# Residual spill behind two more loads, and the first pair of block products made ready inside the opening, in a two-block transformer kernel on Trainium2

## The reference, cut to what matters

```python
def rms_norm(x, g):
    y = x * lax.rsqrt(jnp.mean(x * x, axis=-1, keepdims=True) + RMS_EPS)
    return y * g
...
x = x + rms_norm(mixed @ w_out[l], norm_mix_post[l])
h = rms_norm(x, norm_ffn_pre[l])
f = (jax.nn.silu(h @ w_ffn_gate[l]) * (h @ w_ffn_up[l])) @ w_ffn_down[l]
x = x + rms_norm(f, norm_ffn_post[l])
```

## Time and profile before

| | |
|---|---|
| median of 3 runs | 1445.99 us (1445.91 to 1446.22) |
| the profiled execution's own time | 1444.36 us |
| its span | 1442.6 us |
| TensorE busy | 1414.1 us, 98% |
| VectorE, ScalarE, GpSimd busy | 812.2, 716.8 and 793.2 us |
| DMA | 143.03 MB, 99 GB/s over the span |
| granted TensorE clock, mean | 0.995 |

### The profile page before, as it was taken

How to read it: one execution, slowest core, us unless ns; L and a number is a source line. 1 busy time by engine, 2 the same in 40 slices (tenths; PEclk the granted TensorE clock), 3 DMA queues, 4 the chain that set the end, 5 groups by cost and what they waited for, 6 DMA issues and landing times.

```text
span 1442.6 us, 22205 instructions
## 1 busy us (share of the span) xinstructions
PE 1414.1 (98%) x8248; PEld 1207.4 (84%) x8248; DVE 812.2 (56%) x1426; ACT 716.8 (50%) x1254; POOL 793.2 (55%) x462
## 2 busy tenths in 40 slices
PE   9999999999999988899999999999999999999999
PEld 7888888888788767799998887877677899999887
DVE  6425656776525266676763345888765667764000
ACT  5143435665644235566652225665666566664221
POOL 4434323762344426877764456766237877775443
PEclk9999999999999999999999999999999999999999
DMA  6423312122133322332324333422124423233433
GB/s 204 137 87 88 88 59 59 45 60 59 52 97 100 97 108 78 113 117 89 118 86 148 105 110 126 127 74 59 45 73 146 124 96 118 91 115 117 126 108 117
DMA packets 40050, 143.03 MB, mean 99 GB/s; under 512 B 4656, under 2 KB 4912, under 8 KB 39696
## 3 DMA queue, kind: packets, MB, share of 16 engines
q1 hardware_dynamic: 38688, 139.08, 31.0%
q10 hardware_dynamic: 1264, 2.62, 0.6%
HBM read 135.40 MB, written 6.29 MB: 98 GB/s over the span
## 4 chain that ended last, share of the span: by engine, by line
PE 87%; DVE 5%; POOL 3%; ACT 2%; issue 2%; DMA 1%; SPq 0%; DVEq 0%; ACTq 0%; POOLq 0%
PE bank L1596 10%; PE bank L1598 10%; PE bank L1597 10%; PE bank L1949 8%; PE bank L1951 8%; PE bank L1950 8%; PE bank L1625 3%; PE bank L1627 3%; PE bank L1626 3%; PE bank L2053 3%; PE bank L2055 2%; PE bank L2054 2%; PE bank L1843 1%; PE bank L1878 1%; PE bank L1863 1%
## 5 line engine op out<-in xcount | busy, mean ns | idle before, releaser
L671 POOL TENSOR_TENSOR wL<-raw,wH 128x1024 fp32r<-128x1024 f32 x165 | 404.8, 2453 | 518.9 <-ACT wH L848 387.4
L848 ACT ACTIVATE wH<-raw 128x1024 fp32r<-128x1024 f32 x136 | 143.7, 1057 | 322.3 <-PE bank L1598 251.2
L1596 PE MATMUL bank<-aH,wH 128*128 128x512 f32 x376 | 150.1, 399 | 14.3 <-POOL wL L671 14.3
L1597 PE MATMUL bank<-aL,wH 128*128 128x512 f32 x376 | 147.7, 393 | 0.0
L1598 PE MATMUL bank<-aH,wL 128*128 128x512 f32 x376 | 147.6, 393 | 0.0
L1596 PE MATMUL bank<-fH,wH 128*128 128x512 f32 x352 | 137.1, 389 | 0.0
L1598 PE MATMUL bank<-fH,wL 128*128 128x512 f32 x352 | 137.1, 389 | 0.0
L1597 PE MATMUL bank<-fL,wH 128*128 128x512 f32 x352 | 137.0, 389 | 0.0
L1949 PE MATMUL bank<-aH,wH 128*128 128x256 f32 x408 | 115.3, 283 | 0.0
L1951 PE MATMUL bank<-aH,wL 128*128 128x256 f32 x408 | 115.3, 283 | 0.0
L1950 PE MATMUL bank<-aL,wH 128*128 128x256 f32 x408 | 115.2, 282 | 0.0
(11 more groups left out here) (456 smaller groups left out, 3844.8 us busy)
## 6 DMA issues: line engine op xcount, KB each, us to landing
raw<-in_w SPq DMA_DIRECT2D x200, 512.0 KB, 3.6
raw_too<-in_w SPq DMA_DIRECT2D x34, 512.0 KB, 3.8
kept_x<-xT SPq DMA_DIRECT2D x2, 2048.0 KB, 9.2
xT<-kept_x SPq DMA_DIRECT2D x8, 512.0 KB, 4.9
bmk<-in_bias SPq DMA_DIRECT2D x6, 512.0 KB, 4.7
out_x<-xT SPq DMA_DIRECT2D x8, 256.0 KB, 4.6
xT<-in_x SPq DMA_DIRECT2D x3, 512.0 KB, 7.0
ct<-in_ct ACTq DMA_DIRECT2D x3, 384.0 KB, 3.7
```

The costliest lines, as they stand in the source:

```text
L671: pool.tensor_tensor(wL[:, c_slot, :], raw[:, c_slot, :], wH[:, c_slot, :].bitcast(F32), ALU.subtract).then_inc(sem("w_lo"), 1)
L848: act.activation(wH[:, s, :], raw[:, s, :], ACT.Copy).then_inc(sem("w_hi"), 1)
L1596: pe.matmul(bank[:], hi, H[:, ka, :], start=(k == 0), stop=False)
L1597: pe.matmul(bank[:], hi, L[:, ka, :], start=False, stop=False)
```

## The change

Both gu stages are changed in the same way, as far as the first has it differently from the second.

1. **Spill.** The store of the residual is cut into two halves of 1 MB. In gu1 they stand behind loads 5 and 6 of the phase, in gu2 behind loads 3 and 4; before, one store of 2 MB stood behind load 3.
2. **y_work.** The tile is moved in memory (fH is placed first), and in gu1 the eight `y_made` copies are issued one by one behind the copies that make aH, before the squares; before, they stood in two groups of four behind the first and the second feature. gu2 had them early already.
3. **POOL in gu1.** The four `t_sum` and three `t_low` are put one by one between the lows of chunks 3 to 10; before, they came from chunk 7 on, some in twos. In gu2 the `t_low`s move one chunk back. The `t_high`s on ACT follow.
4. **First pair.** It lands in raw_too instead of raw (all pairs change slots), and its loads wait for the spill and for the users of xT instead of for the lows of the last two opening chunks. Its x11 is split before the last chunk's copy, its x21 copied, s1 and s3 split before x12, and p5(0) is computed between p1(0) and p2(0) instead of between p1(1) and p4(0). ACT's `keep_u2(0)` stands ahead of the copy of pair 1's x21.
5. **Down phase.** Since the last pair now lies in raw, the first two chunks of dn wait for its s4 and its x22 instead of for those of the pair before it.

Core of the diff (orders of waits in `pair_orders` follow the code and are left out, as is the matching reorder in DVE's `swiglu`, which takes s1's low and s4 of pair 0 ahead of the loop):

```diff
@@ two_blocks_kernel @@
+            fH = sb("fH", [P, KF, S], F32R, ffn)
             with ExitStack() as over:
-                sb("under_y", [P, KF - KD, S], F32, over)
+                sb("under_y", [P, KF - 2 * KD, S], F32, over)
                 y_work = sb("y_work", [P, KD, S], F32, over)
-            fH = sb("fH", [P, KF, S], F32R, ffn)
...
-            return raw_too[:, tile, :] if j % 2 else raw[:, (early + tile) % 2, :]
+            return raw[:, (early + tile) % 2, :] if j % 2 else raw_too[:, tile, :]
@@ SP, pair_loads @@
-                for tile in range(2):
-                    sp.wait_ge(sem("w_lo"), p.c0 + p.nt - 1 + tile)
-                    pair_load(p, 0, tile)
-                sp.wait_ge(sem("stored"), 16 * (stage_of(p) + 1))
+                sp.wait_ge(sem("stored"), 32 * (stage_of(p) + 1))
                 sp.wait_ge(sem("pair_act"), after("y_made", KD * (stage_of(p) + 1)))
...
@@ SP, down_loads @@
+                    if c == 0:
+                        sp.wait_ge(sem("pair_dve"), after("s4", done))
+                    if c == 1:
+                        sp.wait_ge(sem("pair_pool"), after("lo_x22", done))
@@ SP, openings @@
-                        if t == 3:
+                        if t in ((5, 6) if p.name == "gu1" else (3, 4)):
...
-                            sp.dma_start(kept, xT[:].rearrange("p a s -> p (a s)")).then_inc(sem("stored"), 16)
+                            kt = 0 if t in (3, 5) else KD // 2
+                            sp.dma_start(kept[:, kt * S:(kt + KD // 2) * S], xT[:, kt:kt + KD // 2, :].rearrange("p a s -> p (a s)"))\
+                                .then_inc(sem("stored"), 16)
@@ ACT, before gu1 @@
-            high_of_x("h2", "g_ffn_pre", "res1", None, kts=range(0, 4))
-            ahead(PH["gu1"], 0)
-            high_of_x("h2", "g_ffn_pre", "res1", None, kts=range(4, 6))
-            ahead(PH["gu1"], 1)
-            high_of_x("h2", "g_ffn_pre", "res1", None, kts=range(6, KD))
+            for kt in range(KD):
+                high_of_x("h2", "g_ffn_pre", "res1", None, kts=[kt])
+                if kt in (3, 5):
+                    ahead(PH["gu1"], (kt - 3) // 2)
+                y_made(PH["gu1"], [kt])
@@ TensorE, pairs @@
                 p1(0)
+                pe.wait_ge(sem("pair_pool"), after("t_lo", 3 * stage_of(p) + 1))
+                p5(0)
                 p2(0)
-                pe.wait_ge(sem("pair_pool"), after("t_lo", 3 * (stage_of(p) + 1)))
+                pe.wait_ge(sem("pair_pool"), after("t_lo", 3 * stage_of(p) + 3))
                 p6(0)
                 p7(0)
                 for j in range(1, n):
                     p1(j)
-                    p5(j - 1)
-                    if j == 1:
+                    if j > 1:
+                        p5(j - 1)
+                    else:
                         pe.wait_ge(sem("pair_dve"), after("t4_lo", stage_of(p) + 1))
```

More of the change, by code:

```diff
@@ L596, in pair_loads @@
                     pair_load(p, j, 0)
-                    sp.wait_ge(sem("pair_act"), after("xc", base + j))
+                    if j >= 1:
+                        sp.wait_ge(sem("pair_act"), after("xc", base + j))
+                    if j == 1:
+                        sp.wait_ge(sem("w_lo"), p.c0 + p.nt)
                     if j >= 2:
@@ L610, in down_loads @@
                         if c == 2:
-                            sp.wait_ge(sem("pair_pe"), after("p3", PAIRS_BEFORE[gu.name] + PAIRS[gu.name]))
+                            sp.wait_ge(sem("pair_pe"), after("p3", done))
                         kt = 2 * (c - 2)
@@ L776, in _ @@
             p = PH["gu1"]
-            for t in range(2, p.nt):
-                opening_chunk(p, t)
-                if t >= 7:
-                    {7: lambda: t_sum(p, 1), 8: lambda: t_sum(p, 3), 9: lambda: t_sum(p, 2),
-                     10: lambda: (t_sum(p, 4), t_low(p, 1, 1)), 11: lambda: (t_low(p, 2, 3), t_low(p, 3, 2))}[t]()
+            opening_chunk(p, 2)
+            opening_chunk(p, 3)
+            t_sum(p, 1)
+            opening_chunk(p, 4)
+            t_sum(p, 3)
+            opening_chunk(p, 5)
+            t_sum(p, 2)
+            opening_chunk(p, 6)
+            t_sum(p, 4)
+            opening_chunk(p, 7)
+            t_low(p, 1, 1)
+            opening_chunk(p, 8)
+            t_low(p, 2, 3)
+            opening_chunk(p, 9)
+            t_low(p, 3, 2)
+            opening_chunk(p, 10)
+            opening_chunk(p, 11)
             pairs(p)
@@ L913, in high_of_x, with y_made @@
                     square(norm * KD + kt, lambda: xT[:, kt, :])
+            def y_made(p, kts):
+                gain = ("g_ffn_pre", "g_norm2")[stage_of(p)]
+                for kt in kts:
+                    act.activation(y_work[:, kt, :], xT[:, kt, :], ACT.Copy, scale=vec(gain, kt)).then_inc(sem("pair_act"), 1)
             def load_constants(part):
@@ L1189, in high_f @@
                 act.activation(fH[:, j, :], tmp[:, j % 2, :] if src is None else src[:], ACT.Copy).then_inc(sem("ff_fH"), 1)
-            def y_made(p, kts):
-                gain = ("g_ffn_pre", "g_norm2")[stage_of(p)]
-                for kt in kts:
-                    act.activation(y_work[:, kt, :], xT[:, kt, :], ACT.Copy, scale=vec(gain, kt)).then_inc(sem("pair_act"), 1)
             def t_high(p, n, i):
@@ L1565, in _ @@
             silu(p, 2)
+            high_x11(PAIRS_BEFORE["gu2"], 0)
             ahead(p, 5)
```

78 lines of the change are left out of this document (38 added, 40 removed).

## The result

The changed kernel takes **1426.41 us** (median of 4 runs, 1425.42 to 1429.55), the kernel before, beside it, 1445.95 (4 runs). The ratio is 0.9872, 95% interval 0.9853 to 0.9891: 19.5 us less, 16 to 21 by the interval. The forecast was 1430.5 with a range of 1425 to 1438. The profiled execution took 1427.21 us, its span is 1425.4.

A forecast was written before the change was run, and what follows sets the result against it. TensorE, busy 98%, bounds the kernel; its waits lie mostly in gu1's opening. 15.1 + 1.7 - 0.2 = 16.6, less 1.1 for seams, from 1444.36 gives 1428.9; plus 1.6 to the median, 1430.5 us, range 1425 to 1438.

The forecast's parts named there:

- (a): gu1 opening, tile 4: spill behind two more loads removes the 7.0 us wait for chunk 4 and 2.1 of lower clock.
- 9.1 us: gu1 opening: the spill's 7.0 us wait plus 2.1 lower clock; the predicted win at tile 5 was 5.1 instead.
- (b): gu1 opening: y_made copies before the squares no longer delay chunk 8's copy, which made TensorE wait 2.97 us.
- (c): gu1 opening: earlier t_sums on POOL block DVE's adds; +0.4 at x lows, 2.7 us at the sum, +0.9 before tile 5.
- (d): gu1 tiles 6 to 11: POOL nearly keeps pace; 0.5 us for waits, 1.0 for lower clock or a seam.
- The rival that POOL becomes the bound: gu1 opening: tiles 6 to 11 each wait some 0.8 more; 5 us more or less, 1433 to 1438; chance 0.27.
- (e): gu1 first pair: earlier readiness and new order cut p7's wait from 2.2 to 0.6, p4(0) +0.5; gu1 wins 15.1 us.
- (f): gu2: 0.25 us won before tile 5, nt_ wait falls from 2.1 to 0.6; 1.7 won in all.
- (g): Down stages: turned slots delay chunk 0's load; price 0 to 1.3 us per stage, 0.1 each taken.
- the 1.1 us then taken off for seams: TensorE's restarts after some five waits, each costing 0.1 to 0.4 beyond the wait; lowers 16.6 to 15.5 us.

The follow-up runs named there:

- e2: Kernel before with only the spill halved and moved behind later loads in both gu stages; 1439.37 us, ratio 0.9956.
- e1: Changed kernel with both spill halves put back behind load 3 in gu1 only; 1432.20 us, ratio 0.9905 to before.
- e3: Changed kernel with all of POOL's t operations in gu1's opening but the first t_sum one chunk later; 1423.58 us.
- e4: Changed kernel with all seven of POOL's t operations in gu1's opening two chunks later; 1423.51 us.
- the run with full clock: Changed kernel with ACT's high copy of chunk 5 ahead of the silu of tile 1 in gu2; 1423.87 us.
- e8: Changed kernel with POOL's t operations two chunks later in gu1, gu2's chunk 5 copy before the silu, x21's copy before u2_kept; 1421.71 us.
- e10: The kernel of e8 with the three t_lows in gu1's opening one chunk later still; 1423.18 us.
- e9: Kernel before with only ACT's u2_kept moved ahead of the copy of x21 in each first pair; 1443.22 us, ratio 0.9984.
- e6: Changed kernel with the first pair's p5(0) put back between p1(1) and p4(0); 1426.84 us.

## Why the prediction was right, and where it was not

**The spill (a).** Right in its times: after, less the 1.57 us by which gu1 begins later, has ACT's copy of chunk 4 at 522.5 (predicted 522.6), load 6 at 526.1 (526.2), tile 4 at 526.8 (527.0). The "9.1 us" were the price of the spill in the kernel before alone: e2 shows 9.3 up to p1(0), and 7.8 over the stage. Beside the rest it is 4.3 (e1). The prediction had the overlap in its sum (5.1 at tile 5, not 9.1).

**y_made (b).** The chunk 8 copy waits no more for ACT; tile 8's 2.97 us is a seam of 0.1. It does not go with the spill alone (2.81 in e2) and is gone with the rest alone (e1). No run separates the y_made copies from POOL's order there.

**The lock of DVE and POOL (c).** Right: 2.7 predicted at the sum, 2.49 measured; the sum at 534.4, measured 534.2 (535.81 - 1.57). As predicted one add ends before t_sum 3 is over and seven behind it, these in 5.3 us (7 x 0.75 was 5.25). At the last x low 0.4 was predicted, 0.16 measured. In front of tile 5 I had 0.9 of wait; the run with full clock shows 0.63, the profiled one lower clock in its place, and tile 5 at 537.4 instead of 537.0. The remedy followed from the term: e3 and e4 take 3.0 and 3.95 us away.

**Tiles 6 to 11 (d).** I put 0.5 for POOL and 1.0 for clock or a seam. From tile 5 to p1(0) after takes 38.85 us where seven tiles take 38.1: 0.8 in all, most of it tiles of 5.64. The lower clock came, but at the end of tile 4 and not in these tiles, so that tile 5 was 0.4 late and the 1.5 here 0.7 too much; the two nearly cancel. p1(0) at 576.2 (577.80 - 1.57) was predicted at 576.5. The rival that POOL becomes the bound was right as to mechanism (e8, e10), but at 0.2 us a tile, not 0.8.

**First pair (e).** Waits 0.56 and 0.34 against 0.6 and 0.5; p4(0) at 586.1 against 586.2; gu1 wins 15.2 against 15.1. Two reasons were too simple: the order of u2_kept gives 1.1 of the 1.6 and not all (e9), and p6 finds the kept p1 ready in gu1 also without the new place of p5(0) (e6).

**gu2 (f) and the slots (g).** 1.57 in the products and 0.32 at tile 5 against 1.7 in all. The cost of the slots turned round, 0.1 each, is none. ACT in after, at the end of gu1:

```profile
735.23 1.06 ACT L1292 ACTIVATE wH<-raw 128x1024 fp32r<-128x1024 f32 x1 [0.24 <-DMA raw<-in_w]
736.19 0.36 ACT L1285 ACTIVATE ssum<-bank 128x256 f32<-128x256 f32 x1
```

ACT waits 0.24 us for the chunk's landing, u3_kept ends at 736.55, and the p4 that needs it starts at 737.13, unhindered.

**The sum.** 15.1 + 1.7 - 0.2 = 16.6 was made, 17.1 measured. The step that was mis-sized is the 1.1 us then taken off for seams: the terms had been read as places in time, from the start of one tile to that of another, and held the seams already. That is 1.1 of the 4.1 us between 1430.5 and 1426.41. Then 0.5 is the sum's own, and 2.4 the step from a profiled run to a median: 1.6 was added, since before had it above its profiled run, while after's median lies 0.8 below its own; with the rounding, that is all. None of this was a mechanism; the 2.4 lie within what single runs of one kernel differ by (1425.42 to 1429.55 for after). That the profiled span shows the stages' 17.1 as 17.2 is chance: gu1 began 1.57 later, and 1.6 were given back by the clock of a stretch that the change does not touch.

## What to carry to other kernels

Read the price of a fix on the timeline of the fixed kernel, not as the wait in the old one: two fixes that free the same engine one behind the other overlap (7.8 + 10.9 gave 15.2), since the delays on the other engines that the first one's wait had covered become due. And read a wait together with the clock before it: a tile that runs slow waits less for the next chunk, and the distance from start to start tells whether anything was lost. Filling an idle engine is not free where it shares a port: before POOL's work is moved into a hole, look which DVE operations with two SBUF inputs lie in that hole, and whether a reduction that TensorE waits for ends with them; here seven operations two chunks later were worth 3.95 us. And before an idle time is counted as room, see what ended it: where it was a chain of splits across two engines, the room moved away with the work.
